# A two-block transformer on one core: layer ends, mixing front and latent attention in another order, with unread products ahead of three runs of weight products

## The reference

```python
def swiglu(x, w_in, w_out):
    gate, up = jnp.split(x @ w_in, 2, axis=-1)
    return (jax.nn.silu(gate) * up) @ w_out
# first_block, for layer in range(2); m is the RWKV mix in layer 0, window attention in layer 1
    h = h + 0.5 * rms_norm(swiglu(rms_norm(h, g[0]), ...), g[1])
    u = rms_norm(h, g[2])
    h = h + rms_norm(m, g[3])
    h = h + 0.5 * rms_norm(swiglu(rms_norm(h, g[4]), ...), g[5])
# rwkv7_time_mix
    x_prev = jnp.pad(x, ((0, 0), (1, 0), (0, 0)))[:, :-1]
    xx = x_prev - x
    xr, xw, xk, xv, xa, xg = [x + xx * mu[i] for i in range(6)]
    r = xr @ w_rkv[0]; k = xk @ w_rkv[1]; v = xv @ w_rkv[2]
    w = -jax.nn.softplus(-(w0 + jnp.tanh(xw @ w1) @ w2)) - 0.5
    a = jax.nn.sigmoid(a0 + (xa @ a1) @ a2)
# second_block: shift, scale, gate from c @ w_ada; h = rmsnorm(x) * (1 + scale) + shift; proj = h @ w_in
    q = rmsnorm(c_q, q_norm_gain) @ w_uq            # 8 heads of 64 + 32 (rotated)
    kv = rmsnorm(c_kv, kv_norm_gain) @ w_ukv        # keys 64, values 64 of each head
    o_b = latent_attention(q_nope, q_pe, k_nope, k_pe, v_b)
    merged = sigmoid(g_a) * y_a + sigmoid(g_b) * y_b; x = x + gate * (merged @ w_out)
```

## Time and profile before

| | |
|---|---|
| time, median of 3 runs | 2803.5 us (2800.75 to 2810.16) |
| profiled execution | 2804.03 us, its span 2802.2 us |
| mean granted clock of PE | 0.978 of full |
| busy of PE, DVE, ACT, POOL | 2670.2, 1121.8, 633.5, 1768.9 us |

### The profile page before, as it was taken

One profiled execution on the slowest core, in us unless ns is written; L12 is line 12 of the kernel. 1 busy time (PEld: TensorE's weight loads), 2 busy tenths in 40 slices (PEclk: granted clock), 3 DMA queues, 4 the chain that ended last, 5 costly groups with the idle time before them and its releaser, 6 DMA issues.

```text
span 2802.2 us, 47886 instructions
## 1 busy us (share of the span) xinstructions
PE 2670.2 (95%) x17904; PEld 2168.6 (77%) x17904; DVE 1121.8 (40%) x1651; ACT 633.5 (23%) x1213; POOL 1768.9 (63%) x1795
## 2 busy tenths in 40 slices
PE   8999998988887999999999999999999999999998
PEld 7888876767775788888888888778888878777677
DVE  3333036874554533310633312775333232123344
ACT  2111025433432211100311101443111011353211
POOL 6777675773321577777577776675777757645565
PEclk9999999989998999999999999999999999999998
DMA  4333322220000233333233332432333323222212
GB/s 138 97 94 97 94 73 71 75 57 4 4 4 16 72 90 94 97 94 98 71 95 97 94 97 84 151 125 70 96 97 94 98 69 103 83 60 72 73 46 79
DMA packets 116792, 225.94 MB, mean 81 GB/s; under 512 B 13088, under 2 KB 13856, under 8 KB 115616
## 3 DMA queue, kind: packets, MB, share of 16 engines
q1 hardware_dynamic: 114624, 209.46, 25.9%
q10 hardware_dynamic: 2016, 14.22, 1.4%
HBM read 221.53 MB, written 2.10 MB: 80 GB/s over the span
## 4 chain that ended last, share of the span: by engine, by line
PE 84%; DVE 9%; ACT 3%; issue 2%; POOL 1%; DMA 1%; SPq 0%; DVEq 0%; ACTq 0%; POOLq 0%
PE bank L222 21%; PE bank L224 21%; PE bank L223 21%; PE bank L326 1%; DVE acc L322 1%; PE bank L1330 1%; DVE h L705 1%; PE bank L1862 1%; PE bank L240 1%; PE bank L241 1%; PE bank L244 1%; DVE x_lo L1090 1%; PE bank L1345 1%; PE bank L2296 1%; PE bank L2287 1%
## 5 line engine op out<-in xcount | busy, mean ns | idle before, releaser
L209 POOL TENSOR_TENSOR w_lo<-w_raw,w_hi 128x512 fp32r<-128x512 f32 x778 | 1046.8, 1345 | 761.6 <-PE bank L224 613.3
L222 PE MATMUL bank<-x_hi,w_hi 128*128 128x512 f32 x1904 | 752.5, 395 | 12.6 <-issue 5.3
L224 PE MATMUL bank<-x_hi,w_lo 128*128 128x512 f32 x1904 | 749.5, 394 | 0.0
L223 PE MATMUL bank<-x_lo,w_hi 128*128 128x512 f32 x1904 | 748.0, 393 | 0.0
L214 POOL TENSOR_SCALAR w_hi<-w_raw 128x512 fp32r<-128x512 f32 x778 | 579.3, 745 | 4.9 <-DMA w_raw<-weights 4.9
L222 PEld LDWEIGHTS bank<-x_hi,w_hi 128*128 128x128 f32 x1904 | 359.4, 189 | 98.9 <-issue 9.0
L223 PEld LDWEIGHTS bank<-x_lo,w_hi 128*128 128x128 f32 x1904 | 359.6, 189 | 78.6 <-issue 0.2
L224 PEld LDWEIGHTS bank<-x_hi,w_lo 128*128 128x128 f32 x1904 | 359.3, 189 | 77.9
L670 DVE TENSOR_TENSOR f<-bank,rstd 128x512 f32<-128x512 f32 x88 | 56.7, 686 | 596.6 <-PE bank L224 589.0
L224 PE MATMUL bank<-mid_hi,w_lo 128*128 128x512 f32 x704 | 276.0, 392 | 0.0
L223 PE MATMUL bank<-mid_lo,w_hi 128*128 128x512 f32 x704 | 275.6, 392 | 0.0
(11 more groups left out here) (438 smaller groups left out, 3513.3 us busy)
## 6 DMA issues: line engine op xcount, KB each, us to landing
w_raw<-weights SPq DMA_DIRECT2D x778, 256.0 KB, 2.6
ada_w<-ada_in ACTq DMA_DIRECT2D x8, 1536.0 KB, 7.1
h<-xT SPq DMA_DIRECT2D x4, 512.0 KB, 7.1
out<-f SPq DMA_DIRECT2D x8, 256.0 KB, 2.2
mask_b<-mask_b_in ACTq DMA_DIRECT2D x1, 640.0 KB, 4.9
spread<-spread_in SPq DMA_DIRECT2D x1, 512.0 KB, 8.0
window<-window_in ACTq DMA_DIRECT2D x1, 512.0 KB, 3.7
masks<-masks_in SPq DMA_DIRECT2D x1, 320.0 KB, 7.8
```

Source lines behind the costliest of these rows:

```text
L209: pool.tensor_tensor(w_lo[:, (n - 1) % RW, :], w_raw[:, (n - 1) % RS, :], w_hi[:, (n - 1) % RW, :].bitcast(F32), ALU.subtract).then_inc(w_ ...
L222: pe.matmul(outs[m], w_hi[:, s, c], hi, start=first, stop=False)
L223: pe.matmul(outs[m], w_hi[:, s, c], lo, start=False, stop=False)
L224: done = pe.matmul(outs[m], w_lo[:, s, c], hi, start=False, stop=last)
```

## The change

The function `closing_products` takes the last three units of six layer ends together and goes bank by bank; the norm there names tile 7 alone, and DVE adds tile 6 to `acc`. In the front of the mix the keys' first half takes `x_hi` ahead of `x_lo` (`keys_early`), mixing uses four buffers (`mix_at`), `u_arr` is written two tiles ahead, two steps of `lora_in` come after the tiles, ACT copies the second half of the keys two tiles sooner, the low-rank products go by the banks that are free, `v_out(0)` is moved into `factors(5)`, and `r_gather` is written later. The 36 products for `ada` (the vector for shift, scale, gate) are spread differently, ten of them paired with unread ones. In latent attention units and banks are dealt out anew (`BRANCH`), the first half of the keys comes ahead of the second of the queries, three rounds of scores stand between the remaining products, ACT and not DVE copies the values, and four branch units come within the last rounds. Unread products are added ahead of f0 (6), ahead of the keys (12) and in the end of f3 (4 and 7); one of `unread_products` shows as two instructions in the trace, as the L402 do.

```diff
+        def closing_products(pe, outs, hi, lo, n0, tiles):
+
+            ks = range(tiles - CLOSING, tiles)
+            for m, o in enumerate(outs):
+                c = slice(m * P, (m + 1) * P)
+                for k in ks:
+                    if m == 0:
+                        pe.wait_ge(w_lo_ready, n0 + k + 1)
+                    w = (n0 + k) % RW
+                    pe.matmul(o, w_hi[:, w, c], hi[:, k, :], start=False, stop=False)
+                    pe.matmul(o, w_hi[:, w, c], lo[:, k, :], start=False, stop=False)
+                    done = pe.matmul(o, w_lo[:, w, c], hi[:, k, :], start=False, stop=k == tiles - 1)
+                    if m == len(outs) - 1:
+                        done.then_inc(w_used, 1)
+                    elif k == tiles - 1:
+                        done.then_inc(out_ready, 1)
...
-                self.pre, self.post = Norm(KT, ODD), Norm(KT, (6, 7), late=True)
+                self.pre, self.post = Norm(KT, ODD), Norm(KT, (7,), late=True)
...
-                            done = ada_products(pe, 12 + 4 * k, 16 + 4 * k)
-                            if k == 2:
+                        if s.after is not None and k < 7:
+                            done = ada_products(pe, 10 + 2 * k, 12 + 2 * k)
...
+        def mix_at(q):
+
+            return sq[:, q % 2, :] if q % 4 < 2 or q >= KT else (acc, sq_last)[q % 2][:]
...
+            norm_wide(pe, s.pre, sa[3])
+            unread_products(pe, sa[2], 12)
+
+            def keys_early(k):
+                n = s.n_k + k
+                pe.wait_ge(w_lo_ready, n + 1)
+                pe.wait_ge(x_hi_ready, s.x0 + k + 1)
+                for m in range(4):
+                    if k == 0 and m == 3:
+                        pe.wait_ge(rstd_ready, s.rs + 1)
+                    c = slice(m * P, (m + 1) * P)
+                    pe.matmul(sa[m][:], w_hi[:, n % RW, c], x_hi[:, k, :], start=k == 0, stop=False)
+                    pe.matmul(sa[m][:], w_lo[:, n % RW, c], x_hi[:, k, :], start=False, stop=False)
+                pe.wait_ge(x_lo_ready, s.x0 + k + 1)
+                for m in range(4):
+                    done = pe.matmul(sa[m][:], w_hi[:, n % RW, m * P:(m + 1) * P], x_lo[:, k, :], start=False, stop=k == KT - 1)
+                done.then_inc(w_used, 1)
+
+            for k in each:
+                keys_early(k)
...
+            pe.wait_ge(*ra("k", 3))
+            low_rank(0, range(4)).then_inc(w_used, 1)
+            pe.wait_ge(*ra("k", 7))
+            low_rank(1, range(4)).then_inc(w_used, 1)
+            pe.wait_ge(*ra("sg", 0))
+            for k in each:
+                g = slice(32 * (k % 4), 32 * (k % 4) + 32)
+                done = pe.matmul(sa[0][g, :], gather[:, k, :], square_of(k), start=k < 4, stop=k >= 4, skip_group_check=True)
+            done.then_inc(*rp.tell("sums"))
+            pe.wait_ge(*ra("sg", 3))
+            low_rank(2, (1, 2, 3))
+            pe.wait_ge(*ra("sg", 6))
+            low_rank(3, (0, 1, 2))
+            pe.wait_ge(*ra("norm"))
+            low_rank(2, (0,)).then_inc(w_used, 1)
+            pe.wait_ge(*ra("sg", 7))
+            low_rank(3, (3,)).then_inc(w_used, 1)
...
+                elif q >= 4:
+                    act.wait_ge(x_lo_ready, s.x0 + min(q, KT) - 3 + 2 * (q >= KT))
+                act.activation(mix_at(q), u_arr[:, k, 0:T], ACT.Copy, scale=vcol(f"mu{i}", k)).then_inc(mix_ready, 1)
...
-            for q in range(KT, 2 * KT):
+            for q in range(KT, 2 * KT - 2):
                 tile(q)
             act.wait_ge(w_used, s.n_k + 2 * KT)
             for m in range(4):
                 act.activation(k_arr[:, 4 + m, :], bank[SETB][m][:], ACT.Copy).then_inc(*ra.tell("k", 4 + m))
+            for q in range(2 * KT - 2, 2 * KT):
+                tile(q)
...
+            factors(5, lambda: v_out(0))
...
+            for q in range(1, KT):
+                if q + 2 < KT:
+                    u_tile(q + 2)
                 tile(q)
-                if 1 <= q < 7:
-                    lora_in(q - 1)
+                if 2 <= q < 6:
+                    lora_in(q - 2)
+            lora_in(4)
+            lora_in(5)
...
+                for b, k in output[i - STEPS:i - STEPS + 1] if STEPS <= i < STEPS + 4 else output[4:-CLOSING] if i == STEPS + 4 else ():
...
+            closing_products(pe, [o[:] for o in sb_], x_hi, x_lo, s.u1 + KT, KT)
...
-            ada_products(pe, 1, 4)
+            ada_products(pe, 0, 2, unread=True)
             norm_wide(pe, s.post, bank[s.post_at][1])
-            ada_products(pe, 4, 12)
...
+                uk = self.n_gb[1] + KT
+                self.n_uq = self.n_gb[0] + KT, uk + 2
+                self.n_uk = uk, uk + 5
+                self.n_uv = uk + 7
...
             pe.wait_ge(*lv("q", 3))
-            queries(1)
-            for b, set_ in enumerate((sa, sb_)):
-                pe.wait_ge(*(lv("q", 7) if b else pa("gb1", 3)))
-                for k in range(2):
-                    unit_products(pe, [o[:] for o in set_], ckv_hi[:, k, :], ckv_lo[:, k, :], k == 0, k == 1, s.n_uk + 2 * b + k)
-            pe.wait_ge(*lv("k", 3))
+            latent_keys(pe, s, 0, sb_)
+            pe.wait_ge(*pa("gb1", 3))
+            latent_queries(pe, s, 1, sa)
...
+            keys_out(dve, s, 0)
+            queries_out(dve, s, 1)
...
-            pe.wait_ge(*lv("v", TT - 1))
+            pe.wait_ge(*lv("k", 3))
             pe.wait_ge(*la("k"))
+            scores(0)
+            pe.wait_ge(*lv("q", 7))
+            latent_keys(pe, s, 1, bank[SETA])
+            scores(1)
+            pe.wait_ge(*lv("k", 7))
+            for k in range(2):
+                moving_units(pe, bank[SETA], ckv_hi, ckv_lo, k, 2, s.n_uv + k)
+            scores(2)
+            pe.wait_ge(*la("v", TT - 1))
             for i in ROUNDS:
                 for a in head_at(i, 0):
-                    scores(a)
+                    if a >= 3:
+                        scores(a)
                 for r in pair_at(i):
                     values(r)
                 for a in head_at(i, 2):
                     turned_scores(a)
+                if i >= HEADS_B + 1:
+                    for k in ((0,), (1, 2), (3,))[i - HEADS_B - 1]:
+                        branch_unit(pe, s, 0, k)
+
+        BRANCH = (bank[SETB][0:3] + bank[SETA][3:], bank[SETA][0:3] + bank[SETB][3:])
...
-            act.wait_ge(*lv("q", 7))
+            act.wait_ge(w_used, s.n_uq[1] + 3)
...
+                if i == 1:
+                    act.wait_ge(w_used, s.n_uv + 2)
+                    act.wait_ge(rinv_ready, s.kv.index + 1)
+                    for t in range(TT):
+                        act.activation(mla_v[:, t, :], bank[SETA][t][:], ACT.Copy, scale=rinv[:, t:t + 1]).then_inc(*la.tell("v", t))
...
-            dve.wait_ge(w_used, s.n_a)
+            dve.wait_ge(*lv("q", 7))
...
+                if i == 0:
+                    keys_out(dve, s, 1)
...
             blank(pool, 0)
+            for k in each:
+                pool.tensor_scalar(r_gather[:, k, :], gather[:, k, 0:HEADS], vcol("r_k", k), None, ALU.mult).then_inc(*rg.tell("gather", k))
...
+            pe.wait_ge(const_ready, 4)
+            pe.wait_ge(x_hi_ready, 1)
+            unread_products(pe, bank[SETA][2], 6)
```

191 lines of the change are left out of this document (93 added, 98 removed).

## The result

The changed kernel takes 2789.18 us (median of 4 runs, 2780.78 to 2790.11) where the kernel before, on the same chip, takes 2805.13 (4 runs, 2800.75 to 2810.16): a ratio of 0.9936, interval 0.991 to 0.9962. That is 16 us or 0.6% faster. The forecast was 2768 with a range of 2754 to 2783; the direction was right, the gain less than half as large. Run once more against the kernel before, the same code gave 2785.67 (4 runs), ratio 0.9922 [0.9901, 0.9942].

What follows compares the result with a forecast made beforehand. PE was taken as the bound, busy 2670.2 of 2802.2 us, with idle time and half clock recoverable. Terms -1.2 - 8.3 - 15.5 + 0.5 - 11.2 = -35.7 us gave 2768 us, range 2754 to 2783.

Steps and rivals of the forecast that it cites:

- the keys' first half: Front of the mix: taking `x_hi` first lets PE start sooner, DVE holding it at 3.5 us a tile; -9.5 us.
- what follows f3: After f3's end: half clock partly recovered, -1.2 us, against +0.5 for unread products added beside `ada`.
- Start: Ahead of f0: six unread products bring full clock forward for the first eight matmuls; -1.2 us.
- ordinary ends: Ends of the mix, f1, f2 and f3: one group of eight sums and the `acc` wait go; -0.9 us each.
- latent: Latent attention: three waits filled and half clock recovered, -9.5 us; branch units fill a late wait, -1.7; together -11.2.
- The last `w_lo` of the stage ... a stall of 2.1: End of f0: POOL's last `w_lo` comes 2.1 us late, but sums begin near 383.1 in two groups; net -0.5 us.
- Rival (4): Six layer ends: POOL late by a whole unit at each, an end costing 7.6 us; 2812 us, chance 0.02.
- `r_gather: -1.5`: Front of the mix: writing `r_gather` later removes PE's 1.44 us wait for `w_lo` behind it; -1.5 us.
- rival (1): Front of the mix: DVE and POOL shut each other out, 4.2 us a tile, gain 2 not 9.5; 2777 us, chance 0.22.
- Second half and low-rank: Front of the mix: keys' second half keeps its length; earlier copies and bank order in the low-rank part give -3.0 us.
- Values and core: From 502 to 585 us: moving `v_out` removes the 5.4 us wait for `v_arr`, DVE late next; -1.5 us.
- Window attention and behind it: Window attention's end: late `w_lo` but one group less, -0.2 us; behind it recovered half clock, -2.8 us.

Runs made afterwards that it cites:

- first pair: Not a follow-up: the profiled execution of the kernel before (2804.03 us) against the changed kernel's first profiled execution (2780.8 us).
- second pair: Both kernels profiled once more, code unchanged: the kernel before 2803.58 us, the changed kernel 2785.67 us.

## Why the prediction was half right

The way was right and the gain less than half of the one told. Three terms carry most of what is missing: the keys' first half (-9.5 told, -5.2 measured), where DVE's rate was taken too fast; the stretch behind f0 (-1.5 told, +2.8 measured), where the ring that the closing holds was not followed further; and what follows f3 (-0.7 told, +2.9 measured), where clock was counted and a chain of DVE and POOL was the bound.

**Start, ordinary ends, latent: right; f0 right in its number only.** At the start 1.2 was told, and 0.3 and 1.2 came in the two pairs; against the kernel without unread products the six are worth 1.4. An end gives 0.9 as told, less 0.2 to 0.3 that the stretch behind it pays, which I had not reckoned. In f0 0.5 was told and 0.5 came, but the closing by itself made it 1.1 longer: its stall is followed by half clock unless, as it seems, the six products at the start are there too. That the number came out is luck.

Latent gives 7.0 + 4.3 = 11.3 (11.2 told), and the parts are not those told. Ahead of the first turned scores 9.5 was told: half clock went as told, the mask for which I left 0.5 cost PE nothing, and the term put at nothing without a reason was POOL's `turn_b` behind its splits, 2.4. Behind them 1.7 was told and 4.3 came: one of two waits of 1.7 for `prob_b` went, as told, and the other 2.6 are 5.4 us of half clock ahead of the last root, which the first pair's after does not have. Of the twelve executions of changed code seven have none there (137.0), and five have 3.4 to 7.3 us of it (138.7 to 140.5). So 8 to 11 is what latent gives, and 11 is its good case.

**"The last `w_lo` of the stage ... a stall of 2.1": the step ended too early.** The stall was right, and I asked what is late *before* the end, not what the held ring does *behind* it. The closing gives three places back at once, so POOL's splits move 5 to 7 us later, onto DVE's updates: +2.3 (35.4 for 33.1 with the closing alone, 33.3 with two units). Rival (4), closing stalls, came true in small: a stall of 2.0 at f0 and of 2.5 in window attention, none at ordinary ends. (Its time of 2812 does not follow from its own terms: 8.3 lost and 46 added to 2768 make 2822.) `r_gather: -1.5` was a wrong term: it is worth nothing there, and 0.5 the other way. PE's wait of 1.44 behind it was, it seems, only the place where lateness of DVE's chain had shown.

**Keys' first half: -9.5 told, -5.2 measured; rival (1) named the cause, and its size lies halfway.** "28.01 us for eight tiles, 3.5 each with POOL beside it" took DVE's rate with POOL of the earlier trace rows, where POOL worked 20.12 of 39 us. In the new order POOL does the same in 33: 22.00, and each one slows the other more. With POOL's piece taken away 5.6 us more come out, which is more than the missing 4.3: this is the step that failed, DVE's 3.5 us a tile. So the price of overlap grows with what is saved: a rate read in a stretch with gaps is not the rate without them. The clock was told rightly (1.00 from 418 to 451), the unread products had no part in it.

How they slow each other can be read instruction by instruction, as in the rows of f3 above. In the changed kernel's trace 244 DVE instructions (TENSOR_TENSOR, 128 x 512, both inputs in SBUF) update `h`, add to `acc` or write `x_lo` or `mid_lo`. Of them 189 begin while one of POOL's runs, and nine in ten of these end 0.53 to 0.55 us after POOL's has ended; alone they take 0.68. The Trainium skill, page "SBUF — State Buffer", section "Who interferes with whom", has DVE with two SBUF inputs and GpSimd exclude each other, while an operation with one input in PSUM stays free. The trace agrees with both: 675 to 678 ns for the latter whatever POOL does, and for the former a wait for the whole instruction of the other side, which the profile counts into the time of the one that waits. A mean such as 1238 ns is a mix of instructions that waited and others that did not, and depends on how many meet. That is rival (1)'s mechanism; what it overpriced is that all of DVE's instructions would be in it. (Its 4.2 us a tile is not worked out from its rows: the busy sums it names, 28.01 and 20.12, would make 6.0. And the bound of 2786 that I took from (1) and (3) together is 2782 by their own prices.)

**Second half and low-rank: -3.0 told, -4.4 to -5.7 measured; right in kind, its parts not.** "It keeps its length" failed, to the good: from the first copy of one half to that of the other 26.3 us became 20.2, of which the earlier copies are 2.8 (the wait for `k_arr` is 0.87 where it was 3.67), as told, and the rest is PE running through, 20.00 of 20.00 us in the window from 454 to 474. The low-rank part gave nothing: from there to the first `a_arr` 15.7 us became 16.0 and 17.4 (the latter with 3.4 us of half clock), since the wait of 2.60 for `head_a` turned into 3.7 for `r_and_a`, and one of 2.0 for `a_arr` came.

**Values and core: -1.5 and the mix's end -0.9 told; not to be seen.** The wait of 5.4 went, and 4.4 for `w_lo` came, behind the `r_gather` that the same change had put there: I had both in hand ("DVE is late next, and POOL now has `r_gather` here") but priced it within the -1.5. Without that the core starts 5 to 7 us sooner, and it gives that back by its end in the executions that I have. Where in the core it goes is open. Its length differs by 5 us between executions of the same code and by 9.5 among all sixteen; part of that is the clock, of whose lower level there are 48 us from `a_arr` to the end of the mix in the shortest of them (455.0) and 75 in the longest (463.7). What sets it is not shown.

**Window attention and behind it: -0.2 and -2.8 told; +1.0 and -3.1 seen in the first pair, +0.5 and +0.1 in the second.** The other execution of before has hardly any half clock there, so the forecast's -2.8 counted on a loss that the kernel before does not have each time. What the change does do is make it steady: 35.0 nine times of nine, against 38.1 and 34.9 before. How often before has the dip, and so what the change is worth here, two executions do not tell. Inside window attention the stall for `w_lo` was told (2.9, and 2.5 came), but the -0.2 does not follow from my own terms: sums that begin 1.5 later, less one group of 0.94, end 0.5 later. The nine executions take 137.7 to 139.8, where before took 138.8 and 139.0.

**f3 and what follows: -2.1 and +0.5 told; -0.9 and +2.9 came.** Its -1.2 was counted as clock. Clock did come back, and PE then stood still for `x_hi` five times. The bound of the place was the chain of DVE and POOL, which coming early made worse. That the phase in which POOL and DVE meet makes the difference is shown by PE's start alone: nineteen products instead of seven take away all five waits and 2.4 us up to the ninth unit with three closing units, and 3.5 us of the stretch with two. Another part is late release again: the first unit begins 13.8 us behind the root with three closing units and 13.0 with two. POOL alone was not moved.

Together, for the first pair of traces, told less measured: 4.3 behind f0, 4.3 in the keys, 3.6 behind f3, 1.5 in core and mix's end, 1.2 in window attention, 0.8 behind ends and 0.9 at the start make 16.6 us missing; the keys' second half gave 2.7 more and the clock behind window attention 0.3. That is the 13.4 between 35.7 and 22.3, to rounding. The second pair differs by 17.2 us and the medians by 16 and 23, so of the 22.3 a few are luck of that pair: half clock behind window attention (3.0 of it absent in the second) and the short core.

## What to carry to other kernels

When a stage's end holds a ring's places longer to save a few products, follow the producer into the next stage: it will work when the ring lets it, and what it holds up there, or is held up by, pays. Take two closing units before three, and measure them alone: in the kernel before three were worth 0 and two 8 us. In the changed kernel the same step did not show in the whole, with nineteen unread products besides (0.9923 for 0.9936 and 0.9922): it came with half clock behind window attention, and in two of three executions with a slower f2.

Do not price a stretch by an engine's busy time when another engine slows it; ask what the rate becomes when both are packed closer. Do not read such a pair from means: lay the two engines' timelines side by side and see which instruction ends behind which. And do not count a dip of the clock as recoverable from a single execution: look at a second profile of the same kernel first.

## What the runs showed of the hardware

DVE's operation on two SBUF tiles of 128 x 512 takes 0.68 us alone. Begun beside one of POOL's splits it ends about 0.54 us behind that split's end, so that it reads 1.1 to 1.8; begun first it keeps 0.68, and the split that begins beside it waits in the same way (`w_lo` 1.3 alone, up to 1.83; `w_hi` 0.62 alone, 1.06 beside). With one PSUM input DVE keeps 0.68 to 0.74. A DVE copy from SBUF to SBUF took 0.42 alone and 1.52 beside the splits, once.

In some executions f2 takes 376 us and not 369.6: 859 matmuls in 200 us for 876, 233 ns from start to start for 229, with a granted clock of 1.00 and PE never idle. Nothing in the records explains that 2%; it came twice, both times in kernels with two closing units, and not in two others with two. The kernel before had 2796.33 to 2822.47 over 46 runs, which is far more than the terms argued over here.
